# Rotary embedding of a dilated attention: half swap by VectorE's 32-row writes in place of DMAs

## The reference

```python
def rope(t, positions):
    ...
    t1, t2 = t[..., : dim // 2], t[..., dim // 2:]
    rot = jnp.concatenate([-t2, t1], axis=-1)
    return t * cos + rot * sin

def dilated_mixture(q, k, v, positions):
    q = rope(q.reshape(B, S, DIL_HEADS, DIL_HEAD_DIM), positions)
    k = rope(k.reshape(B, S, DIL_HEADS, DIL_HEAD_DIM), positions)
    ...
    for g, (window, dilation) in enumerate(DIL_CONFIGS):   # (128, 1), (512, 4), (2048, 16)
        o, lse = dilated_group(...)
```

## Time and profile before

| | |
|---|---|
| median of 3 runs | 1714.8 us (1714.66 to 1717.17) |
| profiled execution, its own time | 1715.96 us |
| span in the profile | 1714.1 us |
| granted TensorE clock | 0.999 |
| TensorE, VectorE, ScalarE, GpSimd busy | 98%, 43%, 34%, 30% |
| stage of the dilated attention | about 559 to 1157 us |
| swap DMAs | 192 of 64 KB, 2.0 us from issue to landing |

### The profile page before, as it was taken

The page is one execution under the profiler, slowest core; times in us unless marked ns, Lnnn a source line. Parts: engine busy times, 40 slices in busy tenths (PEclk is TensorE's granted clock), DMA queues, the critical chain, the costliest instruction groups (busy, mean ns, idle before and its releaser), DMA issues.

```text
span 1714.1 us, 22710 instructions
## 1 busy us (share of the span) xinstructions
PE 1685.5 (98%) x8753; PEld 1411.7 (82%) x8753; DVE 745.2 (43%) x1486; ACT 588.9 (34%) x1337; POOL 509.1 (30%) x400
## 2 busy tenths in 40 slices
PE   7999999999999999999999999999999999999998
PEld 6778778889878787888978889787787999988886
DVE  4330255334342212344154541535521888855714
ACT  5101456334333103441135310441113777741211
POOL 6125033023333333021220223015313745534310
PEclk9999999999999999999999999999999999999999
DMA  6113012233267422113131222217465535226332
GB/s 205 50 63 109 13 62 70 87 119 94 74 213 270 119 62 59 50 50 85 56 83 38 77 80 58 74 57 265 125 232 160 143 64 139 53 68 212 108 114 98
DMA packets 99293, 178.21 MB, mean 104 GB/s; under 512 B 16201, under 2 KB 36081, under 8 KB 99057
## 3 DMA queue, kind: packets, MB, share of 16 engines
q1 hardware_dynamic: 63280, 95.31, 20.3%
q10 hardware_dynamic: 35904, 81.44, 13.4%
HBM read 115.49 MB, written 48.63 MB: 96 GB/s over the span
## 4 chain that ended last, share of the span: by engine, by line
PE 94%; DVE 2%; DMA 1%; POOL 1%; ACT 1%; issue 0%; SPq 0%; POOLq 0%; DVEq 0%
PE ps L1193 23%; PE ps L1107 14%; PE ps L813 13%; PE ps L1045 5%; PE ps L1360 5%; PE ps L1300 5%; PE ps L1241 4%; PE ps L947 4%; PE ps L1330 4%; PE ps L1313 3%; PE ps L868 3%; PE ps L1209 2%; PE ps L1222 2%; PE ps L999 2%; PE ps L972 1%; PE ps L846 1%
## 5 line engine op out<-in xcount | busy, mean ns | idle before, releaser
L700 POOL TENSOR_SCALAR w_hi<-w_stage 128x1024 fp32r<-128x1024 f32 (+3 forms) x140 | 126.9, 914 | 997.4 <-PE ps L1193 357.0
L707 POOL TENSOR_TENSOR w_lo<-w_stage,w_hi 128x1024 fp32r<-128x1024 f32 (+3 forms) x140 | 270.6, 1941 | 8.9
L1193 PE MATMUL ps<-h2T_hi,w_hi 128*128 128x512 f32 x384 | 156.0, 406 | 0.7 <-ACT gate_tiles L1608 0.7
L1107 PE MATMUL ps<-h2T_hi,w_hi 128*128 128x512 f32 x384 | 154.0, 401 | 0.4 <-issue 0.3
L1193 PE MATMUL ps<-h2T_hi,w_lo 128*128 128x512 f32 x384 | 152.5, 397 | 0.0
L1107 PE MATMUL ps<-h2T_hi,w_lo 128*128 128x512 f32 x384 | 151.6, 395 | 0.0
L1107 PE MATMUL ps<-h2T_lo,w_hi 128*128 128x512 f32 x384 | 151.5, 395 | 0.0
L1193 PE MATMUL ps<-h2T_lo,w_hi 128*128 128x512 f32 x384 | 151.3, 394 | 0.0
L1735 ACT ACTIVATE probs_dil<-probs_dil,dil_stats_out 128x256 f32<-128x256 f32 (+2 forms) x192 | 87.5, 457 | 104.7 <-DVE dil_stats_out L2299 104.7
L1300 PE MATMUL ps<-k_mla,q_mla 128*128 128x512 f32 x384 | 104.3, 407 | 0.0
L2391 DVE TENSOR_REDUCE small<-ps 128x1 f32<-128x1024 f32 x64 | 77.7, 1214 | 55.1 <-PE ps L1300 54.8
(11 more groups left out here) (295 smaller groups left out, 3756.2 us busy)
## 6 DMA issues: line engine op xcount, KB each, us to landing
w_stage<-in_w_in SPq DMA_DIRECT2D x76, 512.0 KB, 3.9
rope_swapped<-rope_in SPq DMA_DIRECT2D x192, 64.0 KB, 2.0
w_stage<-in_w_out SPq DMA_DIRECT2D x16, 512.0 KB, 3.8
gate_scr<-gate_tiles ACTq DMA_DIRECT2D x16, 512.0 KB, 3.7
gates<-gate_scr ACTq DMA_DIRECT2D x32, 256.0 KB, 3.5
dil_scr<-dil_out SPq DMA_DIRECT2D x96, 64.0 KB, 1.6
dil_nums<-dil_scr ACTq DMA_DIRECT2D x24, 256.0 KB, 4.2
x_back<-in_x ACTq DMA_DIRECT2D x8, 512.0 KB, 3.7
```

The lines of the kernel that those rows point to most:

```text
L700: last = nc.gpsimd.tensor_scalar(hi_, raw_, 1.0, 0.0, ALU.mult, ALU.add)
L707: last = nc.gpsimd.tensor_tensor(lo_, raw_, hi_.bitcast(F32), ALU.subtract)
L1107: m = pe.matmul(ps[:, gate_bank(u), :], a[:, s, k, P * m_:P * m_ + P], b[:, k, COLS * n:COLS * n + COLS], start=(k == 0 and j == 0), stop= ...
L1193: m = pe.matmul(bank, a, b, start=(k == 0 and i == 0), stop=(k == KT - 1 and i == 2))
```

## The change

The copy to `ts`, the tile `ts` and the four swap DMAs go. `rope_cos` waits for the product itself. `rope_sin` has four VectorE instructions: each takes a quarter of 32 rows of the product from PSUM, multiplies it by the sine table of the same rows and by -1 (times the queries' scale), and writes it 32 rows up or down into `rot`. The table of the same rows has the opposite sign of the one at the destination, hence the -1. `rot` has two buffers. The bank is given free (`d_read`) after the last quarter and not after the cosine product. For the first step of a group `rope_sin` stands ahead of `d_soft`.

```diff
--- before.py
+++ after.py
@@ -325,8 +325,7 @@
 
     s8 = ExitStack()
     vd = sb("v_dil", [P, TT + 1, COLS], F32, s8)
-    ts = sb("rope_in", [P, COLS], F32, s8)
-    rot = sb("rope_swapped", [P, COLS], F32, s8)
+    rot = sb("rope_swapped", [P, 2, COLS], F32, s8)
     osb = sb("dil_out", [P, 2, G, HD], F32, s8)
     dstat = sb("dil_stats_out", [P, 2, TT, STAT], F32, s8)
     masks = sb("masks", [P, MASK_W + P], F32, s8)
@@ -595,15 +594,6 @@
         def load_chunks(first, end):
             for n in range(first, end):
                 load_chunk(n)
-
-        def swap_halves(u):
-
-            r = rope_units(u)
-            sp.wait_ge(*after("d_copied", r + 1))
-            if r:
-                sp.wait_ge(*after("roped", r))
-            for b in range(4):
-                sp.dma_start(rot[32 * b:32 * b + 32, :], ts[32 * (b ^ 1):32 * (b ^ 1) + 32, :]).then_inc(sem("swapped"), 16)
 
         def d_rows(g, t):
             start, step = tile_start(g, t)
@@ -669,9 +659,6 @@
             u = slot // 2
             if slot % 2 == 0 and u in panel_start:
                 place, start = slot, panel_start[u]
-            done = unit_before(slot)
-            if done and done[3] != "v":
-                swap_halves(done[0])
             if slot - 2 in step_at:
                 g, i = step_at[slot - 2]
                 d_store(g, i)
@@ -1747,18 +1734,13 @@
             done = unit_before(slot)
             if done:
                 u, r, g, kind, t = done
-                if kind == "v" and t == 0:
-                    act.wait_ge(*after("d_read", u))
-                    if g:
-                        act.wait_ge(*after("d_valued", d_step(g, 0)))
-                act.wait_ge(*after("d_done", u + 1))
                 if kind == "v":
+                    if t == 0:
+                        act.wait_ge(*after("d_read", u))
+                        if g:
+                            act.wait_ge(*after("d_valued", d_step(g, 0)))
+                    act.wait_ge(*after("d_done", u + 1))
                     act.activation(vd[:, t, :], ps[:, d_bank(u), :], ACT.Copy).then_inc(sem("d_read"), 1)
-                else:
-                    if r:
-                        act.wait_ge(*after("swapped", 64 * r))
-                    act.activation(ts[:], ps[:, d_bank(u), :], ACT.Copy,
-                                   scale=HD ** -0.5 if kind == "q" else 1.0).then_inc(sem("d_copied"), 1)
             if slot in step_at:
                 d_exp(*step_at[slot])
             if slot == D_SLOTS - 2:
@@ -2270,19 +2252,24 @@
                 dve.wait_ge(*after("d_scored", d_step(g - 1, 4 * j + 4)))
             if kind == "q" and (g or j >= 2):
                 dve.wait_ge(*after("d_scored", d_step(g, 4 * (j - 2) + 4)))
-            dve.wait_ge(*after("d_copied", r + 1))
+            dve.wait_ge(*after("d_done", u + 1))
             nc.vector.scalar_tensor_tensor(rope_dst(g, kind, t), grouped(g, n, ps[:, d_bank(u), :]), HD ** -0.5 if kind == "q" else 1.0,
-                                           grouped(g, n, cosT[:, COLS * n:COLS * n + COLS]), ALU.mult, ALU.mult).then_inc(sem("d_read"), 1)
+                                           grouped(g, n, cosT[:, COLS * n:COLS * n + COLS]), ALU.mult, ALU.mult).then_inc(sem("rope_half"), 1)
 
         def rope_sin(u, r, g, kind, t):
 
             n = t % 2
-            dve.wait_ge(*after("swapped", 64 * (r + 1)))
-            nc.vector.tensor_tensor(rot[:], rot[:], sinT[:, COLS * n:COLS * n + COLS], ALU.mult).then_inc(sem("rope_half"), 1)
+            if r >= 2:
+                dve.wait_ge(*after("roped", r - 1))
+            for b in range(4):
+                out_rows, rows = slice(32 * b, 32 * b + 32), slice(32 * (b ^ 1), 32 * (b ^ 1) + 32)
+                last = nc.vector.scalar_tensor_tensor(rot[out_rows, r % 2, :], ps[rows, d_bank(u), :], -HD ** -0.5 if kind == "q" else -1.0,
+                                                      sinT[rows, COLS * n:COLS * n + COLS], ALU.mult, ALU.mult)
+            last.then_inc(sem("d_read"), 1)
             dve.wait_ge(*after("rope_half", r + 1))
             dve.wait_ge(*after("d_read", u + 1))
             dst = rope_dst(g, kind, t)
-            nc.vector.tensor_tensor(dst, dst, grouped(g, n, rot[:]), ALU.add).then_inc(sem("roped"), 1)
+            nc.vector.tensor_tensor(dst, dst, grouped(g, n, rot[:, r % 2, :]), ALU.add).then_inc(sem("roped"), 1)
 
         def d_soft(g, i):
             n = d_step(g, i)
@@ -2311,14 +2298,17 @@
             done = unit_before(slot)
             rope = done and done[3] != "v"
             if rope:
-                if done[4] == 0 and done[3] == "q":
-                    dve.wait_ge(*after("d_read", done[0]))
                 rope_cos(*done)
+            first = slot in step_at and step_at[slot][1] == 0
+            if rope and first:
+                rope_sin(*done)
             if slot in step_at:
                 d_soft(*step_at[slot])
             if slot - 2 in step_at:
                 d_out(*step_at[slot - 2])
-            if rope:
+            if rope and not first:
+                if done[4] == 0 and done[3] == "q":
+                    dve.wait_ge(*after("d_read", done[0]))
                 rope_sin(*done)
             if slot == D_SLOTS - 2:
                 group_stats = [stats[:, 0], stats[:, 1], dstat[:, 0]]
```

## The result

| | before | after |
|---|---|---|
| median, runs taken side by side (16 each) | 1715.12 us | 1718.37 us |
| ratio after to before | | 1.0019, 95% interval 1.0013 to 1.0026 |
| profiled execution, its own time | 1715.96 us | 1718.44 us |
| span in the profile | 1714.1 us | 1716.7 us |

The change costs 3.25 us, or 0.19%, with an interval of 2.2 to 4.5 us (the ratios times 1715). The forecast was 1716.2 from a before of 1714.8, that is +1.4: right in kind and in range, but less than half of the cost.

A forecast was written before the change was run, and what follows sets the result against it. TensorE's matmul stream was taken as the bound. Late scores in group 2, 0.95 us, plus group starts, 0.4, gave +1.35: 1717.3 us against the profiled execution, 1716.2 on the median; range 1713.5 to 1721.5.

The forecast's parts named there:

- What bounds: Edited stage: a stream of TensorE matmuls; removing waits returns at most about 2 us, VectorE's 89.3 us of DMA waits nothing.
- The price of a quarter: Rotation's sine product on VectorE: four multiplications of 32 rows, 0.73 us apart, 2.92 us to the addition.
- The cheap end: Sine product on VectorE: four overlapping multiplications starting 0.61 us apart, 2.52 us, and 2.56 to the addition.
- rival (1): Sine product: the quarters overlap, 0.61 us apart, nothing is late in group 2; 1714.7 us, chance 0.27.
- the rule that the prediction cited: VectorE: an instruction starting in another group of 32 partitions than the last in that memory waits for all earlier ones; 2.92 us.
- Rival (2): VectorE bounds group 2's query slots: each quarter costs 1.11 us, 15 us in all, 1730 us; chance 0.12.
- Key units, groups 0 and 1: Key units need 5.16 us of VectorE within 5.60; query slots of group 1 keep about 1.5 us; cost 0.
- Steady slots of group 2: Group 2's query slots 138, 140, 142, 144 and 146: scores 0.19 us late each, 0.95 us in all.
- The starts: First steps of groups 1 and 2: late first maximum against earlier addition nearly cancel, 0.2 us each, 0.4 us.
- GpSimd's cost of 0: Beside GpSimd's weight splitting: new multiplications unstretched, additions as exposed as before; cost 0, at most 2.1 us for one meeting.
- Rival (3): Group 2: additions meet GpSimd as chunks come at other times, up to 2.1 us a meeting, 1720.5 us; chance 0.06.
- The sum: Whole kernel: + 0.95 + 0.4 = + 1.35 us, so 1717.3 us against the profiled execution, 1716.2 on the median.

The follow-up runs named there:

- both repairs: Changed kernel with quarters in order 0, 2, 3, 1 and quarters plus addition ahead of the evacuation (first steps: quarters, maxima, addition); 1715.32 us, ratio to before 0.9996.

## Why the prediction was right, and where its sum was short

**What bounds.** Right. TensorE's stream stayed at 98%, the 89 us of VectorE's DMA waits were worth nothing to the end (with one operation of 128 rows and the new order, -0.22 us of stage; with both repairs, -0.35), and the cost lay where VectorE comes too late for a maximum.

**The price of a quarter.** Right. 2.92 us were taken from the evacuation's end to the addition, not counting its first gap; in the trace the quarters are 0.70 apart and last 2.79, with 0.10 to the addition, 2.89. The cheap end, 2.56, fell with rival (1), though it stood nearest on a row: the earlier trace rows shows two operations on the same rows. The trace agrees with the rule that the prediction cited there. Rival (2)'s 1.11 for each was off by far.

**Key units, groups 0 and 1.** Right: cost 0. The later key units show 0.46 to 0.55 us of idling ahead of each cosine product in group 1 and 0.34 in group 2, and no wait for a bank; and the maxima don't make TensorE wait in group 1's steady slots; the earlier trace rows is answered by exponentials released at 901.70 (901.5 forecast), with scores at 903.17.

**Steady slots of group 2.** Right place, five times, but 1.43 us in place of 0.95. The step that failed is "From the addition's start to the end of the last maximum takes 1098.50 - 1096.48 = 2.02 us", a length carried over from before. In after it is 1098.71 to 1100.79, 2.08, and it is made otherwise: the addition is 0.06 shorter, and the maximum behind it doesn't overlap it (0.12). The rule about rows was applied to the quarters only, and not to what follows them two operations later in the same memory. The order 0, 2, 3, 1 gives this back: 5 x 0.12 expected, 0.57 measured, which leaves 0.86 of the forecast 0.95. Slot by slot the pairs aren't alike, as the forecast had them: three are 0.31 to 0.33 late and two 0.23. In the two, as in the pair shown, the scores start 0.06 after the last maximum's end, and 0.19 + 0.06 for the length - 0.03 for the quarters + 0.01 is the 0.23. In the other three they start 0.14 to 0.15 after that end, where the forecast had 0.05 for all from one row; why stays open. These three gaps are worth 0.3 in all. So the 0.86 that seems to bear out the 0.95 is in part luck: without them, 0.6 would be left.

**The starts.** Forecast 0.4, measured 1.29 (0.74 + 0.55; group 0 nothing, as said). The reorder was judged rightly: undone it costs 2.1 us more. The step that failed is "The additions stay as exposed as they are". GpSimd's cost of 0 was argued from the new quarters, which read PSUM and do stay at 0.69, and from slots 138 to 144. But the addition itself moved: without the swap it comes right behind the quarters, into the split of a chunk that it used to miss. Holding the chunks gives 0.86 of it back. In the forecast's terms: it has the third cosine product of group 2 start at 1071.55, 2.66 ahead of the scores (1074.21), and the first maximum at 1076.8, 2.6 behind them. In after, with its scores at 1074.34, and with the chunks held, with scores at 1075.77, they are:

```profile
1072.07 1.18 DVE L2256 SCALAR_TENSOR_TENSOR qT_dil<-ps,cos_table_T 128x512 f32<-128x512 f32 x1
1077.37 0.29 DVE L2286 CUSTOM_DVE_ANT_0 probs_dil<-ps,masks 128x128 f32<-128x128 f32 x1
```

```profile
1073.14 1.14 DVE L2258 SCALAR_TENSOR_TENSOR qT_dil<-ps,cos_table_T 128x512 f32<-128x512 f32 x1 [0.36 <-PE ps L1182]
1078.42 0.29 DVE L2288 CUSTOM_DVE_ANT_0 probs_dil<-ps,masks 128x128 f32<-128x128 f32 x1
```

So in after the product starts only 2.27 ahead, since the long addition keeps VectorE from it, and the maximum comes 3.03 behind; with the chunks held it is 2.63 and 2.65, as forecast. What the starts then still lose, 0.27 and 0.16 us, makes 0.43, nearly the forecast 0.4; but 0.4 was chosen between a loss of 1.8 and a gain of 0.8 and not worked out, so this hit is luck too.

The other order of quarters gives 0.64 back at the same place (0.15 + 0.49). Three more held gaps lie in group 2's chain, behind each of the first two additions and ahead of the first maximum: 0.03 after the end in after, 0.06 to 0.08 before it with the other order. The two repairs can't be added, for their sum of 1.50 is more than the 1.29. In group 2 each brings the first slot from 4.02 back to the 3.64 of before, so there the second finds nothing left. Rival (3) had the mechanism, for group 2's steady slots at 2.1 us a meeting; it is the real one at another place, and about 1 us long. The Trainium skill ("SBUF — State Buffer", section "SBUF: two separate sides") says that the later of the two is blocked until the earlier has ended. The traces agree: the addition that starts in a split ends 0.94 after it (866.71 against 865.77), near its own time of 1.07, and GpSimd's next operation, started at 865.85, takes 1.78 in place of 1.05 and so loses time to the addition in turn.

**The sum.** In the stage: 0.86 where the quarters are late, forecast 0.95; 0.57 for the held maximum, forecast nothing; 1.29 at the starts, forecast 0.4. Together 2.72, against 1.35. The mechanism was right, and its size was short by one neglected gap and one neglected meeting; that the rest comes out so close is in part luck, as said. The total, 3.25 us, is +0.19%: inside the range, and just within the 0.2% that was called "same". The 0.5 between stage and total lies within the measurement's interval.

**What was to be seen.** 192 products at 0.69, 0.70 apart (0.73 forecast); VectorE 91 us busier; no waits for banks. The wait for maxima was forecast at 3 to 4 us and stayed at 2.1, because 1.9 us went to the wait for exponentials behind the same late rotations; both together are 4.0.

**Open.** How the order of quarters and the held chunks overlap in group 1's start (7.45 and 7.13 against 6.86 before), and why three of five steady pairs start 0.09 later behind their maximum, wasn't taken apart. No run combined the chunk hold with the version that has both repairs, whose first additions still take 2.03 and 2.15 us, but in which the last addition ahead of a group's first maxima stands behind them.

## What to carry to other kernels

When a full-width operation is split by rows, every piece waits for the end of the last, and so does the next operation that comes back to that memory on other rows, even two operations later: let the last piece end on the rows from which the next reader starts. Then look what stands behind a wait: work put ahead of an operation that waits for another engine fills its idle time, while behind it it becomes late by its full length. And when a transfer is removed, ask which operation now comes earlier, and what it meets there; an unchanged operation isn't unchanged in cost.

## What the runs showed of the hardware

- VectorE, an operation of 32 rows by 512 fp32 columns from PSUM and SBUF: 0.687 us, the same with and without a shift of 32 rows; 0.415 us for 256 columns and 0.287 for 128.
- On other rows than the last in the same memory, an operation started 0.01 to 0.04 us after the end of the one before (the addition behind the quarters, which also waits for semaphores, 0.10 to 0.11); on the same rows 0.06 to 0.10 before it, with one case of 0.03. The last operation in that memory counts, across one in the other memory.
- An addition with two SBUF inputs took 1.81 to 2.29 us, in the kernels with quarters, when it started inside GpSimd's split of the third chunk, and 1.07 to 1.19 when GpSimd was away. Wherever in the split it started, it ended by its own time less 0.14 us after the split's end: in group 1 0.93 to 0.96 after it (own time 1.08), in group 2 1.02 to 1.06 (1.18), in group 0 0.54 to 0.55 (0.69). The run with one operation, where addition and split of group 1 started together (3.28 us), has 0.95 too. GpSimd's operation behind it took 1.53 to 2.00 in place of 1.05.
- After two TensorE waits of 1.12 and 0.97 us, with 0.7 us of work between them, the granted clock dropped for a few microseconds (matmuls 0.43 apart, which is near the lower of the two levels, 1.2 of 2.4 GHz), and it cost 1.5 us; after waits of 0.31 and 0.96 at the same place it didn't. Eight pieces in place of four showed the same after waits of 0.93 and 0.97: matmuls 0.43 apart from 1082.88 to 1084.16 us. After waits of 0.71 and 0.97 in group 1 of the same run no slot was longer. With sixteen pieces and repeated waits of 2.1 to 4.4 us the granted clock was 0.73 to 0.87 from 1111 to 1200 us, and 1.00 in the 15 us behind, without waits.
